# Opening, layer switch and end of the value stage of a two-layer decoder trunk reordered, with the first two tiles of a layer opened together

## The reference, cut to what matters

```python
def rmsnorm(x, g):
    y = xf * lax.rsqrt(jnp.mean(xf * xf, axis=-1, keepdims=True) + RMS_EPS)
    return (y * g).astype(x.dtype)

h = x                                            # 512 tokens x 1024
for i in range(2):                               # DEPTH
    xn = rmsnorm(h, norm_mix[i])
    proj = xn @ w_in[i]                          # q, k, v, conv B, C, u, pool, gate logits
    ...                                          # attention, conv and pool branches
    h = h + mixed @ w_out[i]
    h = h + peer_ffn(rmsnorm(h, norm_ffn[i]), w_query[i], sub_keys[i], expert_u[i], expert_v[i])
    ple_gate = sigmoid(rmsnorm(h, norm_ple[i]) @ w_ple_gate[i])
    h = h + ple_gate * (p[i] @ w_ple_proj[i])
return h
```

## Time and profile before

| what | us |
|---|---|
| runs: median, lowest, highest | 3835.55, 3833.91, 3837.22 |
| the profiled execution's own time | 3833.89 |
| its span | 3831.8 |
| PE busy (matmuls) | 3789.1 |
| DVE busy | 2870.2 |
| ACT busy | 1445.5 |
| POOL busy | 1500.1 |

### The profile page before, as it was taken

How to read it: one execution, slowest core, us unless ns; L and a number is a source line. 1 busy time by engine, 2 the same in 40 slices (tenths; PEclk the granted TensorE clock), 3 DMA queues, 4 the chain that set the end, 5 groups by cost and what they waited for, 6 DMA issues and landing times.

```text
span 3831.8 us, 53837 instructions
## 1 busy us (share of the span) xinstructions
PE 3789.1 (99%) x17258; PEld 3122.2 (81%) x17258; DVE 2870.2 (75%) x4059; ACT 1445.5 (38%) x1949; POOL 1500.1 (39%) x935
## 2 busy tenths in 40 slices
PE   8999999999999999999999999999999999999998
PEld 6778888888888878888777888888888888788887
DVE  6754659989997278888677546598999973787776
ACT  5443333333333233333455333333333333333334
POOL 1100004444444377777201000044444443786761
PEclk9999999999999999999999999999999999999999
DMA  3223323445555699999322223244555547999993
GB/s 117 82 83 99 99 94 130 147 174 190 189 183 179 208 352 367 362 356 345 131 73 77 93 99 102 86 143 141 175 190 194 192 164 238 352 372 361 343 338 109
DMA packets 325067, 740.37 MB, mean 193 GB/s; under 512 B 30640, under 2 KB 161840, under 8 KB 321584
## 3 DMA queue, kind: packets, MB, share of 16 engines
q1 hardware_dynamic: 105408, 381.73, 28.8%
q10 hardware_dynamic: 174448, 222.40, 17.0%
q0 software_dynamic: 45056, 134.38, 9.6%
HBM read 618.87 MB, written 119.54 MB: 193 GB/s over the span
## 4 chain that ended last, share of the span: by engine, by line
PE 95%; issue 1%; DVE 1%; POOL 1%; ACT 1%; DMA 1%; ACTq 0%; DVEq 0%; POOLq 0%; SPq 0%
PE banks L1284 63%; PE banks L1508 26%; PE banks L1485 2%; PE banks L1346 1%; PE banks L1336 1%; POOL sqs L393 1%; PE banks L1432 1%; PE banks L1355 0%; PE banks L1331 0%; ACT xh L484 0%; POOL hval L426 0%; DMA hval<-early,tail_h 0%; DMA vrow<-in_stream,tail_v 0%; PE banks L1434 0%; DVE qrs L850 0%
## 5 line engine op out<-in xcount | busy, mean ns | idle before, releaser
L1284 PE MATMUL banks<-xh,hi 128*128 128x512 f32 x3264 | 1289.5, 395 | 14.6 <-DVE xl L819 14.6
L1284 PE MATMUL banks<-xl,hi 128*128 128x512 f32 x3264 | 1273.5, 390 | 0.0
L1284 PE MATMUL banks<-xh,lo 128*128 128x512 f32 x3264 | 1271.6, 390 | 0.0
L414 POOL TENSOR_TENSOR lo<-raw,hi 128x1024 fp32r<-128x1024 f32 x240 | 646.2, 2692 | 979.7 <-ACT hi L468 979.5
L807 DVE TENSOR_TENSOR lo<-raw,hi 128x1024 fp32r<-128x1024 f32 x484 | 584.0, 1208 | 398.4 <-ACT hi L468 326.3
L468 ACT ACTIVATE hi<-raw 128x1024 fp32r<-128x1024 f32 x724 | 739.3, 1042 | 278.0 <-DMA raw<-in_stream 177.6
L1284 PEld LDWEIGHTS banks<-xh,hi 128*128 128x128 f32 x3264 | 614.3, 188 | 148.5 <-DVE xl L819 16.7
L1284 PEld LDWEIGHTS banks<-xh,lo 128*128 128x128 f32 x3264 | 613.2, 188 | 130.5
L1284 PEld LDWEIGHTS banks<-xl,hi 128*128 128x128 f32 x3264 | 614.4, 188 | 122.5 <-issue 5.5
L1508 PE MATMUL banks<-hi,ah 128*128 128x512 f32 x1536 | 473.6, 389 | 6.9 <-DVE al L1166 6.9
L1508 PE MATMUL banks<-hi,al 128*128 128x512 f32 x1536 | 473.7, 390 | 0.0
(11 more groups left out here) (217 smaller groups left out, 3413.5 us busy)
## 6 DMA issues: line engine op xcount, KB each, us to landing
raw<-in_stream SPq DMA_DIRECT2D x724, 512.0 KB
early<-eo ACTq DMA_DIRECT2D x256, 256.0 KB, 2.2
gate_table<-stage ACTq DMA_DIRECT2D x24, 2048.0 KB, 6.9
gb<-gate_table ACTq DMA_DIRECT2D x64, 768.0 KB
eb<-early ACTq DMA_DIRECT2D x64, 768.0 KB
vrow<-in_stream,tail_v POOLq DMA_INDIRECT x256
hval<-early,tail_h POOLq DMA_INDIRECT x256
hT<-in_xT ACTq DMA_DIRECT2D x4, 512.0 KB, 8.7
```

The source lines that it names most:

```text
L414: pool.tensor_tensor(lo[k % RING][:, :], raw[k % RAW][:, :], hi[k % RING][:, :].bitcast(f32), ALU.subtract).then_inc(lo_split, 1)
L1284: ins = pe.matmul(out_ap, st[slot][:, a:a + P], mv, start=first and i == 0, stop=last and i == 2)
```

## The change

Four places are rewritten; the rest differs by line numbers alone.

*Opening.* The loads of tiles 2 and 3 wait until the third part of x has landed. ACT's first table load stands before its first wait. Tile 1 is split after the first two chunks. The squares of chunks 4 to 7 go to a buffer of their own (`sq_late`), and DVE adds these four, while POOL adds chunks 0 to 3; the two sums are what `last_sums` adds. PE runs ten matmuls on `ones` before its first wait. The four table loads named below are set by hand.

*Start of each layer.* PE opens tiles 0 and 1 together (`open_two`): chunk c of tile 0, then chunk c of tile 1, with the sums after chunk 5. Tiles 2 and 3 are split by DVE here, ahead of the reciprocal, no more at the end of the layer. The square of the factor (`rs2`) is POOL's, no more ACT's. In the head pairs the table for Sqrt is loaded once, at the end of the pair before.

*End of V.* ACT loads the table for Sqrt before `take_pj`, squares chunk 1 directly after chunk 0 and each following one step earlier, and rounds PLE's tile 1 later. DVE takes the low part of that tile after the low parts of h. PE computes projection 6 two chunks earlier.

*Layer switch.* DVE makes the low part of chunk 6 after the addition to chunk 7, no more between scaling and multiplying. ACT loads the table for Sqrt before rounding tiles 2 and 3.

```diff
@@ SP, load
+                    if r == 2:
+                        sp.wait_ge(x_in[2], 16)
@@ POOL
-            gather_squares(0)
+            gather_squares(0, DC // 2)
             with pool.Fori(0, DEPTH) as l:
+                pool.wait_ge(scale_ready, l + 1)
+                pool.tensor_tensor(rs2[:, :], rs[0][:, :], rs[0][:, :], ALU.mult).then_inc(square_ready, 1)
@@ ACT
+            act.preload_act_table_set("sqrt_and_others")
             act.wait_ge(vec_in, 16)
...
-                if z == 3:
+                if z == 0:
+                    square(0, 0, 0)
                     split(0, 1)
-                for c in range(z * 2, z * 2 + 2):
-                    square(0, 0, c)
+                    square(0, 0, 1)
+                elif z == 1:
+                    square(0, 0, 2)
+                elif z == 2:
+                    square(0, 0, 3)
+                    late_square(4)
+                else:
+                    for c in range(5, DC):
+                        late_square(c)
...
                 root(l, 0)
-                act.wait_ge(scale_ready, l + 1)
-                act.activation(rs2[:, :], rs[0][:, :], ACT.Square).then_inc(square_ready, 1)
...
                         split(l, 8 if h == 0 else 10, b)
+                    act.preload_act_table_set("sqrt_and_others")
                     split(l, 11, b)
 
+                act.preload_act_table_set("sigmoid_and_others")
...
+                act.preload_act_table_set("sqrt_and_others")
                 take_pj(0)
...
                 square(l, 2, 0)
+                square(l, 2, 1)
                 added(3)
                 added(4)
                 take_pj(3)
-                square(l, 2, 1)
-                split(l, N_PT + 1 + AHEAD)
+                square(l, 2, 2)
                 added(5)
                 added(6)
-                square(l, 2, 2)
                 square(l, 2, 3)
+                split(l, N_PT + 1 + AHEAD)
+                square(l, 2, 4)
                 added(7)
-                for c in range(4, DC):
+                for c in range(5, DC):
                     square(l, 2, c)
...
+                act.preload_act_table_set("sqrt_and_others")
                 for m in range(DC - 2, DC):
                     split(l, N_PLE + m + AHEAD)
@@ DVE
+            link(dve.memset(tile0[:, :], float(X_ODD + EG)))
             split(0, 0)
             for z in range(4):
                 dve.wait_ge(x_in[z], 16)
                 for c in range(z * 2, z * 2 + 2):
                     low_h(0, 0, c, 0)
-            for k in range(1, 4):
-                split(0, k)
-            link(dve.memset(tile0[:, :], float(X_ODD + EG)))
+                if z == 0:
+                    split(0, 1)
+            half = sq_late[:, 0, :]
+            dve.wait_ge(sq_ready, 6)
+            link(dve.tensor_tensor(half, half, sq_late[:, 1, :], ALU.add))
+            dve.wait_ge(sq_ready, 7)
+            link(dve.tensor_tensor(half, half, sq_late[:, 2, :], ALU.add))
+            dve.wait_ge(sq_ready, DC)
+            dve.wait_ge(sq_used, 2 + DC // 2)
+            dve.tensor_tensor(sq[:, 1, :], half, sq_late[:, 3, :], ALU.add).then_inc(sq_used, DC // 2 - 1)
             with steps.loop(DEPTH, DVE_LAYER) as l:
                 dve.memset(uc[:, 0:2], 0.0)
                 link(dve.memset(pw[:, :, 0:16], 0.0), True)
+                split(l, 2)
+                split(l, 3)
                 inverse(l, 0)
...
                 low_value(4)
-                split(l, N_PT + 1 + AHEAD)
                 add_values(7)
                 low_value(5)
                 low_value(6)
                 low_value(7)
+                split(l, N_PT + 1 + AHEAD)
...
                     if m == DC - 1:
-                        for c in range(5, DC - 1):
-                            low_next(c)
+                        low_next(DC - 3)
...
                     if m == DC - 1:
-                        low_next(m)
-                for m in range(DC - 2, DC):
-                    split(l, N_PLE + m + AHEAD)
+                        low_next(DC - 2)
+                        low_next(DC - 1)
@@ PE
             pe.wait_ge(const_ready, 1)
+            for _ in range(WARM):
+                pe.matmul(bank[7][:, 0:P], ones[:, :], ones[:, :], start=True, stop=True)
...
+                    def open_two():
+
+                        pe.wait_ge(lo_split, RAW + l * T + 2)
+                        for c in range(DC):
+                            pe.wait_ge(xl_ready, l * (4 * DC) + c + 1)
+                            for k in range(2):
+                                ins = three(bank[k][:, :], (k, c * P), xh[:, c, :], xl[:, c, :], c == 0, c == DC - 1)
+                                if c == DC - 1:
+                                    ins.then_inc(tile_done, 1)
+                            if c == DC - 3:
+                                last_sums(l * 3)
...
-                    taken(-1)
-                    mix(0, 0)
-                    taken(0)
-                    mix(1, 1)
-                    if not first:
+                    if first:
+                        taken(0)
+                        open_two()
+                    else:
+                        taken(-1)
+                        mix(0, 0)
+                        taken(0)
+                        mix(1, 1)
                         ssq(0)
...
                         project(5)
-                    if c == 5:
                         pe.wait_ge(pj_out, (l + 1) * EARLY_PJ)
                         project(6)
+                    if c == 5:
                         project(7)
```

12 lines of the change are left out of this document (7 added, 5 removed).

## The result

| what | before | changed |
|---|---|---|
| median of the runs, us | 3835.62 (3831.66 to 3839.90, 20 runs) | 3842.32 (3836.53 to 3847.86, 20 runs) |
| the profiled execution's own time | 3833.89 | 3840.20 |
| its span | 3831.8 | 3838.4 |

The ratio of the times is 1.0017, with a 95% interval of 1.0011 to 1.0023: slower by 0.17%, 6.7 us. That lies within the 0.2% taken as no change ahead of time, though not within the noise of 20 runs, and it is 15.6 us above the forecast of 3826.7, outside the range.

What follows compares the result with a forecast made beforehand. PE, holding 95% of the chain, was taken to bound the kernel, so only its waits counted. Gains of 3.4 + 3.2 + 1.65 + 0.55 = 8.8 us took 3835.55 to 3826.7 us; the range was 3823.5 to 3830.2.

Steps and rivals of the forecast that it cites:

- Opening: Program start to the first pair's scores: reciprocal at 25.3 in place of 27.04, scores at 42.6, 3.4 us sooner.
- End of V: End of V in each layer: POOL's sum ready sooner, next to no PE wait before the sums; 1.6 us gained per layer.
- Rival 2: End of V: POOL's earlier additions slow two further low parts, so each layer gains 0.3, not 1.6; 3829.3 us, chance 0.17.
- Layer switch: Between the layers: reciprocal 0.7 to 0.75 us sooner, 0.9 for the table load; scores 1.65 us sooner.
- end: End of the program: DVE's two splits go, one low part less before the last multiply, ACT ends last; 0.55 us gained.
- The ten matmuls: Matmuls on ones before PE's first wait, from 3.3 to about 7.6: cost nothing, valued at 0.
- Rival 1: Opening: the ten matmuls on ones keep the clock up through PE's idle time, 4.5 us gained, not 3.4; 3825.6 us, chance 0.2.
- the first paragraph: Whole kernel: PE's waits that matter lie only in three places; some 30 us of opening and about 10 of stalls winnable.
- At nothing: Items valued at no gain: factor's square on POOL, table load at each pair's end, projection 6, later loads 2 and 3.
- Rival 4: Opening: the clock stays at half, 10.8 us slower in all, 3846.3 us; chance 0.03.
- Rival 3: Opening starts late: tile 1 2 us later than thought, or DVE's additions end late; sum 6.8 us, 3828.7 us, chance 0.12.
- rival 5: The order changes nothing on the path; only the ends of V and of the program count, 3.75 us; 3831.8, chance 0.03.

## Why the prediction was wrong

**Opening, 3.4 forecast, 3.12 measured.** First matmul on h 12.68 (12.5), reciprocal 25.81 (25.3), scores 42.85 (42.6). The distance from reciprocal to scores came out at 17.04 where I had 17.3. The step held; the reciprocal was 0.5 us later than I had it, since the root starts 0.6 us behind the sums (24.49 to 25.09), where I had 0.2 for all hand-overs up to the reciprocal. PE waits 1.63 at the scores, a little under the 2 to 3 foretold.

**End of V, 2 × 1.6 forecast, 2 × 2.15 measured.** Right in kind and undersized. I charged two more low parts at 1 us each to POOL's earlier additions, and PE waits in all 0.5 us for low parts in both layers together: the charge was too high. Rival 2, which had them take the gain back, is refuted by the same row. POOL's and ACT's order is as forecast, and the part alone gives the same 2.15.

**Layer switch 1.65, measured 1.74; end 0.55, measured 0.58**, with ACT last.

**The ten matmuls: valued at nothing, and worth nothing.** The clock is up from 7.2 to 10.6, but PE's first product of h comes at 12.68 and runs at 0.43 us a matmul again. Rival 1 falls with that, and with the run without the ten. The Trainium skill (TensorE: Matmul & The Clock Gate, on HAM oscillation) says that an idle TensorE is put back to half clock. The trace agrees: PE is idle from 7.6 to 12.68, and the granted clock is 0.50 from 10.6.

**The step that failed** is the one in the first paragraph: that the stalls that matter "none lies elsewhere than in the opening, at the end of V and at the layer switch". From there the sum of 8.8 us was carried over the remaining 99% of the span as if everything in it moved rigidly. Waits of PE that *are* there were listed; waits that are *almost* there weren't looked for. The third turn had 1.1 us of slack (slots finished at 763.14, PE's turn at 764.23), and the work before it hung on a margin of 0.10 us between two engines that exclude each other. Both could be read from the trace of before, had I asked for DVE's and POOL's timelines ahead of each of PE's fixed waits. The item belonged under "At nothing", with the words "covered by 1.1 us", and a rival of its own beside it: as measured, 4.6 us in each layer, which puts 3826.7 at 3835.9, no gain at all, before any effect on the clock. Which side of the margin the change would fall on couldn't be forecast from the rows of before: it hung on the pause of 0.09 us. The range should have held both.

I had used the rule itself, at V's end only: the Trainium skill (SBUF — State Buffer, Who interferes with whom) says that an instruction of DVE with two SBUF inputs and one of GpSimd that reads SBUF take the shared pair for a whole instruction, the first to start winning, and that a cast can enter the mode that contends as well. The runs agree: 0.29 ahead, 2.53 behind, 2.40 for POOL's instruction itself. That it turns a shift of 0.1 us into one of 4 us is what I didn't draw from it.

**The second step that failed: the clock.** I costed PE's growing wait at the scores as mere waiting ("PE's five microseconds of gain in the two tiles are mostly not banked") and gave the clock a chance of 0.03 in the opening only. The half clock behind waits cost 9.4 us in the ledger of the one profiled execution, as much as the waits at the turns. The other runs bear the size out: the median granted clock is 0.995 in the changed kernel's 20 runs and 0.998 in 31 of the kernel before. "A clock at half after 17, or new waits of PE in later pairs" stood in the text as what would make it wrong, and both came true, the first literally, the second in the experts instead of a pair.

Rival 4, the slower one, had the right sign for a wrong reason: the opening did not stay at half clock. Rival 3 and rival 5 are refuted by the times of the opening above.

**With the collision out of the way the sum holds.** The changed kernel with the turn one tile later has a median of 3826.91, against 3826.7. Part of that is luck: 9.7 us of gains in place of 8.8, less what its own half clocks cost, and a kernel before that was 0.7 us faster in that batch than the 3835.55 of the forecast. Against its own before the gain is 7.9 us, and the interval runs from 4.2 to 11.5.

**What stays open.** What puts the pause of 0.09 us into DVE's batch 31 us ahead of the third selection's cast. It goes with the whole change, in every profile, and the end of V alone doesn't bring it; which other part does no run here tells. And what filler matmuls would give at the wait inside V, where the clock falls in most profiles.

## What to carry to other kernels

Before costing a change as local, look at each point where the bounding engine meets another one: not only at the waits that are there, but at how much is left until one appears; and where two engines exclude each other, read which of them starts first and by how much. A margin of 0.1 us is none: here an edit hundreds of microseconds away flipped it, while another (the end of V alone) did not. Where a local gain is real in the trace and the total is worse, follow one instruction stream through both traces and note where the difference jumps: the cure was here at a place that the change never touched: one number, or three instructions that don't contend moved ahead of one that does. And put filler work where the trace shows the wait, not at the head of the stage that contains it.

## What the runs showed of the hardware

- **A race of 0.1 us worth 16.** 0.27 us of extra work on DVE in each layer made the kernel 15.9 us slower (10 to 21), through a cast blocked for 2.44 instead of 0.29, three products at 4.2 to 4.4 instead of 2.3, two waits of 4.4 us, and half the clock for 6.8 us behind each.
- **The half clock follows a wait, but not in every execution.** Changed, PE waited 1.60 us ahead of the scores at 1948.77 and its clock fell to half from 1949.4 for 6.8 us; the eight scores, 2.39 us before, took 4.03. The kernel with the later turn has the same instructions there and waited 1.63 us (scores at 1946.72), and its clock stayed up. In the kernel before and its variants PE waits 1.9 us at this place, and the clock fell in one profile of six. What decides isn't shown.
- **Runs of one kernel differ by their granted clock.** In 31 runs of the kernel before on one chip, the five with a mean granted clock of 0.999 took 3829.7 to 3833.2 us, and the five with 0.996 took 3838.7 to 3841.4. A single profile can therefore have half-clock stretches that another of the same kernel lacks, worth 1.6 to 3.3 us each in the table above.
- **A memset seems to hold POOL off.** A memset of 128x256 that started 0.02 us ahead of POOL let a cast that started 0.17 us behind POOL go through unblocked, while POOL took 2.65 in place of 2.45. The rows are the same in both layers of one kernel; it was not tested further.
